# Two first layers: attention by pairs of heads on array halves, and gate rows by a transposition, a store and a broadcasting load

## The chip, the core and the metric

The kernel runs on one core of one Trainium2 chip. Its time is device microseconds of one launch, from inputs in HBM to the output in HBM; the comparison is by medians over several runs. TensorE (PE in the profile) does matmuls, VectorE (DVE), ScalarE (ACT) and GpSimd (POOL) the rest, SyncE (SP) issues most of the loads. All data is float32.

## The reference

Two blocks of two layers each work on x of 256 tokens x 1024 features. The changed parts lie in the first block's layers (0 and 1), and in the residual gates of all four layers (0 to 3).

```python
ada = (cond_act @ w_ada + b_ada)[:, None, :]
sh1, sc1, g1, sh2, sc2, g2 = split(ada, 6)            # each 1024 wide
u = layer_norm(x) * (1 + sc1) + sh1
proj = u @ w_in + b_in                                # p, conv b/c/h, mq mk mv, fq fk fv, f_logit, gates
y_moba = attention of 4 heads of 64 on mq, mk, mv     # causal; with 256 tokens one block: plain softmax
y_fox = attention of 4 heads of 64 on fq, fk, fv      # causal, with a forget bias on the logits
gates = sigmoid(gate_logit)                           # 256 x 4096
merged = sum over n of gates[n] * (branches[n] @ w_branch[n])
x = layer_norm(ALPHA * x + g1 * (merged @ w_o)) * ln1_g + ln1_b
u2 = layer_norm(x) * (1 + sc2) + sh2
x = layer_norm(ALPHA * x + g2 * (square(relu(u2 @ w_up + b_up)) @ w_down)) * ln2_g + ln2_b
```

The second block (layers 2 and 3) has an attention layer with 16 head pairs, then a convolution by spectra (Hyena), each followed by a mixture of 16 experts; its two residual sums are `ALPHA * x + g1 * y` and `ALPHA * x + g2 * f` as well. `g1` and `g2` are one number per feature, the same for every token.

## The kernel before

One program of five queues, each written out in order; engines wait for one another by semaphores. Weights come as pieces of 2 MB (128 partitions x 4096) through a ring of six slots, issued by SyncE in a fixed order; a piece is issued when its slot's last reader is done. PSUM has eight banks: six are taken in turn (`take(pe, name)`), two are held (`take(pe, name, hold)`) for attention outputs and for the modulation sums. `emptied` and `wait_evicted` count a bank's evictions.

Modulation (`ada`) of later layers is computed beside other work: VectorE multiplies a weight piece with the condition vector (`mod_step`, or a quarter of it, `mod_part`), transposes in blocks of 32 and sums (`mod_fold`), TensorE sums over partitions with one small matmul (`modulation`, called a fold below), VectorE adds the bias into `modc` (`mod_evict`). `modc[:, L, j]` has feature p of chunk j on partition p: gates 1 are its columns 16 to 23, gates 2 columns 40 to 47.

**Attention of layers 0 and 1** (`attention(L, extra)` in each engine's block). There are 16 units: two kinds, four heads, two query tiles of 128; tile 0 has 128 keys, tile 1 has 256. They are numbered head by head. A step s issues scores of unit s (contraction over 64 partitions, the half of the array where the head lies), transpositions of the probabilities of unit s-2, values of unit s-3 (64 output partitions), and then one product of the gated merge, `gated_branch(l, s)`: eight matmuls of a weight tile with UT and two with a branch output, 256 columns each. VectorE takes the masked maximum (L1947) and scales the probabilities (L1971), ScalarE exponentiates (L1465) and copies the transposed tile out of PSUM (L1473) and makes the gate (L1486). Gated products 16 to 31 follow the attention; product 16 reads the first attention's output, product 24 the second's. After the last one come the output product (`output_product`), which waits for `merged_ready`, the residual sum and norm on VectorE (`finish_tiles`), and the feed-forward part.

**Gate rows.** The residual sum multiplies a PSUM tile of tokens x features with the gate of each feature, so it needs the gates as a row on all partitions (`grow`). `gate_diag` (VectorE, L1829) writes eight 128x128 diagonal matrices with the gates into `diag`; `gate_rows` (TensorE) multiplies all-ones with it, twice 512 columns, into the two held banks; `gate_rows` (ScalarE, L1419 and L1420) copies them to `grow`, halved for gates 1 of layers 0 and 1, and for gates 2 of layers 2 and 3 also into `gsplit`, where each half of the row lies on 64 partitions. This is done eight times and named (L, i) here, i = 0 for gates 1 and 1 for gates 2:

- (0,0), (1,0): TensorE after gated product 31, ahead of the output product
- (0,1), (1,1): TensorE in the down product, after its fourth piece
- (2,0): ahead of the third layer's attention; (3,0): among the Hyena input products
- (2,1), (3,1): at the start of the mixture, ahead of the router

The mixture then runs a loop over the experts, in which VectorE first writes one-hot columns (L2202) that TensorE's gather needs (tile X), and multiplies by `gsplit` at the end of each expert.

GpSimd issues the loads of the norm's rows (`load_lnrow`, L2508 and L2509) after the previous norm, and computes the pooling windows of layers 0 and 1.

Of the kernel before, what the change touches and what calls it, by code (L numbers as in the profile page):

```python
# [26 lines left out]
P = 128  # L27
D = 1024
N = 256
# [26 lines left out]
PAIRS = 16  # L56
RMS_LIMIT = 2.0 ** 32 / P ** 0.5
# [190 lines left out]
def build(nc, a, out):  # L248
    pieces, place = plan_pieces()
    ctx = ExitStack()  # L250
    with ctx:
# [29 lines left out]
        rstd = sb("rstd", [P, TT])  # L281
        smax = sb("smax", [P, 64])
# [61 lines left out]
        SM2, P2, PT2 = view(7936, 2, 512), view(7936, 4, 512), view(9984, 2, 512)  # L344
# [12 lines left out]
        kspec = nc.dram_tensor("filter_spectra", (P, 2, RING), F32, kind="Internal").ap()  # L357
        ftm = acc
# [39 lines left out]
        diag_ready = sem("gate_diagonal_ready")  # L398
# [160 lines left out]
        def attention_steps(us):  # L559


            for s in range(len(us) + 3):
                yield (s if s < len(us) else None,
                       s - 1 if 0 <= s - 1 < len(us) else None,
                       s - 2 if 0 <= s - 2 < len(us) and us[s - 2]["pair"] != 0 else None,
                       s - 3 if 0 <= s - 3 < len(us) and us[s - 3]["pair"] != 0 else None)

        def attention_tiles(L):
            return (SM1, P1, PT1) if L < 2 else (SM2, P2, PT2)

# [4 lines left out]
        def pairs():  # L575

            us = numbered(2)
            return [us[2 * p:2 * p + 2] for p in range(PAIRS)]

# [31 lines left out]
        def _(pe):  # L611
# [31 lines left out]

            def gate_rows(L, i):

                for h in range(2):
                    g = ("rows", L, i, h)
                    bank = take(pe, g, h)
                    pe.wait_ge(diag_ready, 2 * L + i + 1)
                    finish(mm(bank, C("ones"), diag[:, h * 512:h * 512 + 512], True, True), g)  # L650
# [78 lines left out]
            def attention(L, extra=None):  # L729
                us = numbered(L)  # L730
                for s, _, tr, pv in attention_steps(us):
                    if s is not None:
                        u = us[s]
                        g = ("s",) + u["name"]
                        bank = take(pe, g)
# [14 lines left out]
                    if pv is not None:  # L750
                        u = us[pv]
                        if u["first"]:
                            take(pe, ("o", L, u["name"][1], u["hold"]), u["hold"])
# [1981 lines left out]
```

## Time and profile before

| | |
|---|---|
| median of 3 runs | 2474.4 us (2473.87 to 2475.06) |
| the profiled execution | 2474.91 us, of which the span is 2472.9 |
| PE busy | 2322.6 us, 94% of the span, mean granted clock 0.986 |
| DVE, ACT, POOL busy | 1017.7, 356.3, 31.8 us |
| DMA | 701 MB, mean 283 GB/s; 428 to 430 GB/s in most of the expert loops |

Line 615 is the helper through which nearly all matmuls are issued, so tiles and shapes tell them apart, not the line. In the timeline a row is a run of equal instructions: start, length, engine, line, operation, output and input tiles, shape, count; in brackets the idle time before it and what ended it. A float32 matmul is two instructions. `64*128` is a matmul that contracts over 64 partitions, `128*64` one with 64 output partitions. The last instruction of a run is shown with its full latency, so lengths overlap: the time a run occupies is best read from start to next start.

### The profile page before, as it was taken

What the parts mean: (1) busy time and instruction counts of PE and PEld (TensorE: products, weight loads), DVE (VectorE), ACT (ScalarE), POOL (GpSimd) and SP (SyncE); (2) the same over time, 40 slices, a digit from 0 to 9 for tenths busy, and PEclk for the clock granted to TensorE, in tenths of its full rate; (3) what the DMA queues carried; (4) which work ended last, traced back from release to release, by engine and by line L of the source; (5) the groups of instructions that cost most, each with busy time, mean ns of one, the idle gap of its engine ahead of it and who ended that gap; (6) DMA issues with size and microseconds to landing.
All of it is one profiled execution on the core that took longest, in us unless ns stands there. A gap on an engine that the chain in (4) does not pass through costs nothing.

```text
span 2472.9 us, 26320 instructions
## 1 busy us (share of the span) xinstructions
PE 2322.6 (94%) x10448; PEld 1373.8 (56%) x10448; DVE 1017.7 (41%) x2212; ACT 356.3 (14%) x725; POOL 31.8 (1%) x54
## 2 busy tenths in 40 slices
PE   6999999999999999999998998988899989989997
PEld 5878688458878685467554333333397533333332
DVE  4254656767556567223743111111245521111112
ACT  1211111001211110101532111111100011111111
POOL 0100000002000000000000000000000000000000
PEclk9999999999999999999998999999999989999999
DMA  9644868856267688532045999999954369999996
GB/s 313 255 153 171 306 248 291 305 193 234 98 248 257 218 326 303 187 119 85 35 185 228 430 429 429 428 429 428 417 197 170 122 241 429 429 428 429 428 429 290
DMA packets 160900, 701.04 MB, mean 283 GB/s; under 512 B 6064, under 2 KB 15536, under 8 KB 135216
## 3 DMA queue, kind: packets, MB, share of 16 engines
q1 hardware_dynamic: 158512, 691.49, 70.9%
q0 software_dynamic: 2304, 8.39, 1.0%
q8 instruction: 58, 0.95, 0.2%
q14 instruction: 26, 0.21, 0.0%
HBM read 694.61 MB, written 5.24 MB: 283 GB/s over the span
## 4 chain that ended last, share of the span: by engine, by line
PE 73%; DMA 20%; DVE 3%; ACT 2%; issue 1%; SPq 1%; DVEq 0%; ACTq 0%
PE banks L615 72%; DMA ring<-in_exp_w_down_dram 19%; ACT UT L1406 1%; DMA ring<-in_w_ada_dram 1%; PE banks L680 0%; DVE acc L1790 0%; PE banks L748 0%; DVE acc L1763 0%; ACT arena L1613 0%; SPq L2587 0%; DVE arena L2220 0%; DVE arena L2213 0%; DVE X L1872 0%; PE banks L1153 0%; PE banks L995 0%
## 5 line engine op out<-in xcount | busy, mean ns | idle before, releaser
L615 PE MATMUL banks<-ring,arena 128*64 128x512 f32 (+2 forms) x3776 | 976.4, 593 | 80.0 <-DVE arena L2220 29.1
L615 PE MATMUL banks<-UT,ring 128*128 128x256 f32 (+1 forms) x3696 | 729.3, 356 | 7.0 <-ACT UT L1406 3.9
L615 PEld LDWEIGHTS banks<-ring,arena 128*64 128x64 f32 (+1 forms) x3776 | 360.5, 147 | 660.2 <-issue 619.5
L615 PEld LDWEIGHTS banks<-UT,ring 128*128 128x128 f32 x3696 | 623.7, 192 | 86.9 <-issue 15.9
L1790 DVE SCALAR_TENSOR_TENSOR acc<-ring,cact,acc 128x512 f32<-128x512 f32 x280 | 212.7, 760 | 9.9
L2212 DVE TENSOR_TENSOR arena<-arena,banks 128x512 f32<-128x512 f32 x32 | 33.9, 1061 | 442.0 <-PE banks L615 442.0
L1586 ACT ACTIVATE arena<-banks 128x512 f32<-128x512 f32 (+1 forms) x96 | 65.2, 679 | 799.0 <-PE banks L615 759.9
L615 PE MATMUL banks<-arena 64*128 64x512 f32 (+4 forms) x752 | 139.5, 433 | 4.6 <-ACT arena L1453 2.8
L615 PEld LDWEIGHTS banks<-arena 64*128 64x128 f32 (+2 forms) x752 | 69.1, 172 | 77.9 <-issue 62.1
L2220 DVE TENSOR_TENSOR arena<-banks,acc 128x512 f32<-128x512 f32 x32 | 22.2, 692 | 208.7 <-PE banks L615 208.7
L615 PE MATMUL banks<-ring,XN 128*128 128x512 f32 (+1 forms) x192 | 73.0, 540 | 0.0
L615 PE MATMUL banks<-arena,ring 128*128 128x256 f32 x256 | 65.7, 379 | 0.0
L615 PE MATMUL banks<-X,arena 128*64 128x512 f32 x272 | 64.3, 593 | 1.4 <-DVE arena L2170 1.4
L2213 DVE COPY arena<-banks 128x512 f32<-128x512 f32 x32 | 22.2, 692 | 104.6 <-PE banks L995 104.6
L1883 DVE TENSOR_TENSOR arena<-banks,grow 128x512 f32<-128x512 f32 x24 | 16.6, 690 | 117.4 <-PE banks L615 117.3
L615 PE MATMUL banks<-ring,UT 128*128 128x256 f32 (+2 forms) x256 | 62.6, 394 | 0.0
L615 PE MATMUL banks<-XN,ring 128*128 128x512 f32 (+1 forms) x176 | 60.8, 498 | 0.0
L615 PEld LDWEIGHTS banks<-ring,XN 128*128 128x128 f32 x192 | 34.6, 193 | 38.9 <-issue 38.8
L615 PEld LDWEIGHTS banks<-ring,UT 128*128 128x128 f32 x256 | 46.0, 190 | 13.3 <-issue 8.4
L1549 ACT ACTIVATE arena<-banks,small 128x256 f32<-128x256 f32 x64 | 26.9, 471 | 181.3 <-PE banks L615 181.3
L2095 DVE TENSOR_TENSOR arena<-arena 128x512 f32<-128x512 f32 x32 | 21.8, 687 | 74.9 <-ACT arena L1549 74.9
L615 PEld LDWEIGHTS banks<-arena,ring 128*128 128x128 f32 x256 | 48.6, 190 | 6.6
(249 smaller groups left out, 1453.1 us busy)
## 6 DMA issues: line engine op xcount, KB each, us to landing
ring<-in_exp_w_gate_dram SPq DMA_DIRECT2D x64, 2048.0 KB, 22.1
ring<-in_exp_w_up_dram SPq DMA_DIRECT2D x64, 2048.0 KB, 25.2
ring<-in_exp_w_down_dram SPq DMA_DIRECT2D x64, 2048.0 KB, 17.1
ring<-in_w_in_dram SPq DMA_DIRECT2D x26, 2048.0 KB, 14.0
ring<-in_mod_w_dram SPq DMA_DIRECT2D x24, 2048.0 KB, 9.2
ring<-in_w_ada_dram SPq DMA_DIRECT2D x20, 2048.0 KB, 8.5
ring<-in_w_up_dram SPq DMA_DIRECT2D x16, 2048.0 KB, 9.4
ring<-in_w_down_dram SPq DMA_DIRECT2D x16, 2048.0 KB, 9.3
```

Source lines behind the costliest of these rows:

```text
L615: return nc.tensor.matmul(o, lhs, rhs, start=start, stop=stop)
L1406: x = A(dst[:, k, t * P:t * P + P], bank[:, c * P:c * P + P], ACT.Identity, bias=cols[:, shift + k:shift + k + 1], scale=cols[:, shift + 8 ...
L1549: x = A(rt[:, i % 2, c * N:c * N + N], bank[:, c * N:c * N + N], ACT.Relu, bias=S(f"bup{l}", 2 * i + c, 1))
L1586: A(dst, src, func).then_inc(m["g_evicted"][b], 1)
L1790: link(V.scalar_tensor_tensor(out=dst, in0=w[:, k, :], scalar=cact[:, c0 + k:c0 + k + 1], in1=dst, op0=ALU.mult, op1=ALU.add))
L1883: emptied(V.tensor_tensor(tmp[:, hf, :], bank, grow[:, hf * 512:hf * 512 + 512], ALU.mult), g)
L2095: V.tensor_tensor(HID[:, 2 * i:2 * i + 2, :].rearrange("p c n -> p (c n)"), rt[:, i % 2, :], rt[:, i % 2, :], ALU.mult).then_inc(hid_ready, 1)
L2212: done(V.tensor_tensor(quarters_back(G), by_column(SG), by_column(bank), ALU.mult), "up")
L2213: done(V.tensor_copy(HS.rearrange("p j s -> p (j s)"), start("hidden", e)), "hidden")
L2220: done(V.tensor_tensor(YS, start("down", e), gsplit, ALU.mult), "down")
```

## The change

Attention in layers 0 and 1 works on pairs of heads. The units are numbered so that two heads on the two halves of the partitions, of the same query tile, follow each other. A pair step p issues both units' scores, gated product 2p, both units' transpositions of pair p-1, gated product 2p+1, both units' values of pair p-1, with the two heads' matmuls alternating key tile by key tile. In the ninth step there are no scores; gated products 16 and 17 take the two places, and TensorE waits ahead of them for ScalarE's copy of the first attention's output. VectorE and ScalarE follow the same order.

Gate rows are made without TensorE and ScalarE. VectorE transposes 32 columns of `modc` in blocks of 32 into `grows` (for layers 2 and 3 all four at the start of the third layer). GpSimd stores the eight rows of each of the four blocks to HBM (four stores of 8 x 128 bytes, 4 KB in all), waits for them and for the previous norm, and loads the 4 KB back to all 128 partitions (512 KB); for (2,1) and (3,1) two more loads of 128 KB fill `gsplit`. The halving moves into the residual sum, whose multiplication becomes a three-operand one.

```diff
-                    for h in range(4):
-                        b = (h % 2) * HD
-                        for i in range(TT):
+                    for h2, i, r in itertools.product(range(2), range(TT), range(2)):
+                            h, b = 2 * h2 + r, r * HD
...
+            def head_scores(two):
+                held = [take(pe, ("s",) + u["name"]) for u in two]
+                for bank, u in zip(held, two):
+                    x = mm(bank[:, 0:u["nk"]], u["q"], u["keys"][0][1], True, True)
+                    finish(x, ("s",) + u["name"])
...
+            def head_weigh(l, two):
...
+                for t in range(len(two[0]["values"])):
+                    for u in two:
+                        p0, p1, col = u["at"]
+                        x = mm(bank[p0:p1, col:col + P], u["values"][t], PT1[:, u["n"] % 2, t * P:t * P + P],
+                               t == 0, t == len(u["values"]) - 1)
...
+            def attention(l):                                   # TensorE
+                two = head_pairs(l)
+                for p in range(HEAD_PAIRS + 1):
+                    if p < HEAD_PAIRS:
+                        head_scores(two[p])
+                    else:
+                        wait_evicted(pe, ("o", l, 0, 0))
+                    gated_branch(l, 2 * p)
+                    if p:
+                        head_turn(l, two[p - 1])
+                    gated_branch(l, 2 * p + 1)
+                    if p:
+                        head_weigh(l, two[p - 1])
...
-                attention(l, lambda s: gated_branch(l, s))
-                for i in range(16, 32):
+                attention(l)
+                for i in range(18, 32):
                     gated_branch(l, i)
-                gate_rows(l, 0)
...
+            def attention(l):                                   # ScalarE
...
+                    if p < HEAD_PAIRS:
...                      (exponents of both units)
+                    else:
+                        head_out(l, 0)
+                    gate(l, 2 * p)
...                      (copies of both transposed tiles of pair p-1)
+                    gate(l, 2 * p + 1)
+                head_out(l, 1)
...
+            def attention(l):                                   # VectorE
+                two = head_pairs(l)
+                for p in range(HEAD_PAIRS):
+                    for u in two[p]:
+                        head_largest(u)
+                    if p:
+                        gated_branch(l, 2 * p - 1)
+                    mod_part(MOD_SLOTS["in", l, 5 + p // 2], 2 * (p % 2))
+                    for u in two[p]:
+                        head_probabilities(u)
+                    gated_branch(l, 2 * p)
+                    mod_part(MOD_SLOTS["in", l, 5 + p // 2], 2 * (p % 2) + 1)
+                gated_branch(l, 15)
+                mod_evict(MOD_SLOTS["in", l, 8])
...
-            def gate_diag(L, i):
...
+            def gate_turn(L, i):
+                V.transpose(grows[:, 2 * L + i, :], modc[:, L, 16 * i:16 * i + 32]).then_inc(gate_turned, 1)
...
             def finish_tiles(name, gate, tmp, k, plain=None, between=None):
-                wait_evicted(dve, ("rows",) + gate + (1,))
+                dve.wait_ge(grow_loaded, 16 * (2 * gate[0] + gate[1] + 1))
...
-                        emptied(V.tensor_tensor(tmp[:, hf, :], bank, grow[:, hf * 512:hf * 512 + 512], ALU.mult), g)
+                        emptied(V.scalar_tensor_tensor(out=tmp[:, hf, :], in0=bank, scalar=0.5 if gate in ((0, 0), (1, 0)) else 1.0,
+                                                       in1=grow[:, hf * 512:hf * 512 + 512], op0=ALU.mult, op1=ALU.mult), g)
...
-                wait_evicted(dve, ("rows", L, 1, 1))            # mixture, ahead of the expert loop
+                dve.wait_ge(grow_loaded, 16 * (2 * L + 2))
+                dve.wait_ge(gsplit_loaded, 32 * (L - 1))
...
+            def gate_row(L, i):                                 # GpSimd
+                n = 2 * L + i
+                pool.wait_ge(gate_turned, n + 1)
+                c = 16 + 8 * i
+                row = gate_rows[n].rearrange("(c q n) -> q c n", q=4, n=32)
+                for q in range(4):
+                    G.dma_start(row[q], grows[32 * q + c:32 * q + c + 8, n, :]).then_inc(gate_stored, 16)
+                if n:
+                    pool.wait_ge(x_ready, 2 * n)
+                pool.wait_ge(gate_stored, 64 * (n + 1))
+                G.dma_start(grow[:, :], gate_rows[n].partition_broadcast(P)).then_inc(grow_loaded, 16)
+                if L >= 2 and i:
+                    for h in range(2):
+                        G.dma_start(gsplit[h * CAP:h * CAP + CAP, :],
+                                    gate_rows[n][512 * h:512 * h + 512].partition_broadcast(CAP)).then_inc(gsplit_loaded, 16)
...
                 load_lnrow(2 * L)
                 if L < 2:
                     windows(L)
+                gate_row(L, 0)
                 load_lnrow(2 * L + 1)
+                gate_row(L, 1)
```

All calls of `gate_rows` on TensorE and ScalarE and of `gate_diag` on VectorE are gone. `head_largest` and `head_probabilities` are the two halves of VectorE's old step, for one unit each.

## Rows read from the trace of the kernel before

**Rows 1.** The page: shares of the chain that ended last, by engine.
```profile
PE 73%; DMA 20%; DVE 3%; ACT 2%; issue 1%; SPq 1%; DVEq 0%; ACTq 0%
```

**Rows 2.** Stretches: length, busy us and count of PE, PEld, DVE, ACT, POOL, PEclk, DMA share, GB/s.
```profile
117.20:210.70 93.50, 93.35 (x431) 72.69 (x430) 56.48 (x164) 19.36 (x68) 0.00 (x0) 1.00 0.37 132
210.70:281.00 70.30, 70.13 (x328) 61.77 (x328) 37.05 (x78) 8.17 (x18) 0.00 (x0) 1.00 0.76 280
1327.20:1786.00 458.80, 421.88 (x1952) 151.17 (x1952) 80.15 (x175) 53.13 (x64) 0.00 (x0) 1.00 0.99 418
```

**Rows 3.** Timeline of TensorE in the attention of layer 0.
```profile
132.26 0.70 PE L615 MATMUL banks<-arena 64*128 64x256 f32 x2
132.89 0.44 PE L748 MATMUL banks<-const,arena 128*128 128x128 f32 x2
...
138.14 0.48 PE L615 MATMUL banks<-arena 64*128 64x128 f32 x2
...
143.91 0.70 PE L615 MATMUL banks<-arena 64*128 64x256 f32 x2
```

**Rows 4.** Timeline of TensorE in the attention of layer 2.
```profile
1264.66 1.13 PE L615 MATMUL banks<-arena 64*128 64x256 f32 x8
1265.73 1.98 PE L615 MATMUL banks<-XN,ring 128*128 128x512 f32 x4
1267.55 1.04 PE L1153 MATMUL banks<-const,arena 128*128 128x128 f32 x8
1268.42 1.90 PE L615 MATMUL banks<-UT,ring 128*128 128x512 f32 x4
1270.29 1.09 PE L615 MATMUL banks<-arena 128*64 128x128 f32 x16
1271.32 5.42 PE L615 MATMUL banks<-ring,arena 128*128 128x512 f32 x12
```

**Rows 5.** Timeline of VectorE in the attention of layer 0.
```profile
169.46 0.48 DVE L1804 TENSOR_SCALAR acc<-ring,cact 128x512 f32<-128x512 f32 x1 [5.46 <-DMA ring<-in_w_ada_dram]
```

**Rows 6.** Timelines of TensorE and VectorE at (0,0), and TensorE ahead of the down product.
```profile
280.58 0.29 PE L615 MATMUL banks<-folded,const 128*128 128x16 f32 x2
281.80 0.42 DVE L1986 TENSOR_TENSOR XN<-XN,arena 128x256 f32<-128x256 f32 x1
283.56 3.58 PE L615 MATMUL banks<-diag,const 128*128 128x512 f32 x4 [2.69 <-DVE modc L1742]
286.93 13.62 PE L615 MATMUL banks<-ring,XN 128*128 128x512 f32 x31
...
435.33 4.96 PE L615 MATMUL banks<-ring,arena 128*128 128x512 f32 x11 [1.73 <-DVE arena L2095]
```

**Rows 7.** The stretch of the gate-row matmuls at (0,0).
```profile
283.56:286.93 3.37, 3.37 (x4) 1.31 (x5) 3.23 (x5) 0.60 (x1) 0.00 (x0) 0.54 1.04 405
```

**Rows 8.** Timelines at (0,1), (3,0), (2,0) and (2,1).
```profile
491.01 0.29 PE L615 MATMUL banks<-folded,const 128*128 128x16 f32 x2
...
493.88 6.60 PE L615 MATMUL banks<-ring,arena 128*128 128x512 f32 x15
...
1829.05 1.88 PE L615 MATMUL banks<-diag,const 128*128 128x512 f32 x4
...
1177.43 1.29 DVE L2279 TENSOR_REDUCE smax<-banks 128x1 f32<-128x512 f32 x2
...
1306.56 0.16 DVE L1849 RECIPROCAL rstd<-std 128x1 f32<-128x1 f32 x1 [1.67 <-ACT std L1443]
```

**Rows 9.** GpSimd's loads (x, KB, us to landing: all, at 1800 us), and VectorE's diagonal for (0,0).
```profile
lnrow<-in_ln_g_dram POOLq DMA_DIRECT2D x8, 512.0 KB, 4.1
lnrow<-in_ln_b_dram POOLq DMA_DIRECT2D x1, 512.0 KB, 8.1
255.36 1.65 DVE L1829 TENSOR_SCALAR diag<-const,modc 128x128 f32<-128x128 f32 x8
```

**Rows 10.** Timeline of TensorE in the first expert of layer 2: the gather.
```profile
1342.68 1.89 PE L615 MATMUL banks<-X,arena 128*64 128x512 f32 x8
```

More of the change, by code:

```diff
@@ L557, in build @@
         TURN_BASE = {0: 0, 1: 16, 2: 32}
[L559 to L569, printed above, removed]
         def prob_slot(L, u):
@@ L578, in pairs, with head_pairs @@
             return [us[2 * p:2 * p + 2] for p in range(PAIRS)]
+        def head_pairs(l):
+            us = numbered(l)
+            return [us[2 * p:2 * p + 2] for p in range(HEAD_PAIRS)]
         def turns(p, two):
@@ new lines, in head_scores, with head_turn @@
+            def head_scores(two):
[3 more added lines that the diff above has]
+                    finish(x, ("s",) + u["name"])
+            def head_turn(l, two):
+                for u in two:
+                    g = ("t",) + u["name"]
+                    bank = take(pe, g)
+                    pe.wait_ge(prob_ready, UNIT_BASE[l] + u["n"] + 1)
+                    for k in range(u["nk"] // P):
+                        x = nc.tensor.transpose(bank[:, k * P:k * P + P], P1[:, u["n"] % 4, k * P:k * P + P], C("ident"))
+                    finish(x, g)
@@ new lines, in head_weigh @@
+            def head_weigh(l, two):
+                if two[0]["first"]:
+                    take(pe, ("o", l, two[0]["name"][1], two[0]["hold"]), two[0]["hold"])
+                bank = banks[:, BANKS + two[0]["hold"], :]
+                for u in two:
+                    wait_evicted(pe, ("t",) + u["name"])
+                for t in range(len(two[0]["values"])):
+                    for u in two:
+                        p0, p1, col = u["at"]
+                        x = mm(bank[p0:p1, col:col + P], u["values"][t], PT1[:, u["n"] % 2, t * P:t * P + P],
+                               t == 0, t == len(u["values"]) - 1)
+                if two[1]["last"]:
+                    finish(x, ("o", l, two[1]["name"][1], two[1]["hold"]))
@@ L1408, in modulate_tile @@
                     emptied(x, (name, t, h))
-            def gate_rows(L, i, scale=1.0):
-                if 2 * L + i:
-                    act.wait_ge(x_ready, 2 * (2 * L + i))
-                for h in range(2):
-                    g = ("rows", L, i, h)
-                    bank = filled(act, g)
-                    if L >= 2 and i == 1:
-                        own = slice(h * CAP, h * CAP + CAP)
-                        A(gsplit[own, :], bank[own, :], ACT.Copy)
-                    emptied(A(grow[:, h * 512:h * 512 + 512], bank, ACT.Copy, scale=scale), g)
             def first_share(n):
@@ L2362, in attention_block @@
                 mod_evict(len(MOD_STEPS))
-                gate_diag(2, 0)
+                wait_evicted(dve, ("ada", 3, 11, "x"))
+                for L, i in itertools.product((2, 3), range(2)):
+                    gate_turn(L, i)
                 modulate(("h", 2), UT, 2, 0)
```

191 lines of the change are left out of this document (48 added, 143 removed).

## The prediction, made before the changed kernel had run

> **What bounds the kernel now.** First the page. TensorE is busy 94% of the span and the chain that ended last is 73% TensorE and 20% DMA [rows 1]: the kernel is one line of matmuls, and in parts a line of loads. The table by stretch says which parts [rows 2]. In the attention of layer 0 (117.2 to 210.7 us) TensorE is full at granted clock 1.00 while DMA has a share of 0.37; in the second half of the gated product it is full again, with DMA at 0.76. The expert loop (1327.2 to 1786.0) has DMA at 0.99: it is the loads. There the second expert's loads are issued only when the first expert's products have read their slots, so the loop begins when TensorE gets to it: what TensorE saves ahead of a loop moves the whole loop, and what it saves in a loop is worth nothing. Every edit here is ahead of one.
>
> Next the timeline of TensorE in that attention [rows 3]. Two steps (one unit with 256 keys, one with 128) take from 132.26 to 143.91, 11.65 us. Gated products between other gated products take 70.1/16 = 4.38 us each with their share of the folds [rows 2], 4.33 without. So 11.65 - 8.66 = 3.0 us of two steps is attention. Its instruction time is less: two instructions a matmul, 0.213 us each for 256 columns, 0.107 for 128, is 0.64 for scores, 0.64 for values, 0.32 for three transpositions, 1.6 in all. The other 1.4 us are the joints: each burst has a start of the next 0.15 to 0.2 us later than its instructions need (one score of 256 keys: 132.26 to 132.89 is 0.63 for 0.43).
>
> The pair scheme that the third layer already uses shows what becomes of both [rows 4]: two heads' scores, eight instructions of 256 columns, take 1.06 us from start to start where one after the other would be 8 x 0.213 = 1.70; sixteen value instructions of 128 columns on two halves take 1.03 instead of 1.71; eight transpositions take 0.87.
>
> **The change part by part.** *Attention, per layer.* Before: 93.5 us less 16 x 4.33 leaves 24.2 us that are not gated products (four folds, 0.84, among them). After, for each of 8 pairs: scores are four instructions, of which the second head's first overlaps the first head's last; the 5 slots for 8 of [rows 4] make 3 slots for 4, 0.64 for 256 keys and 0.32 for 128, mean 0.48, plus 0.15 for the joint. Values are 4 or 8 instructions at 1.03/16 = 0.064, mean 0.39, plus 0.15. Transpositions are 2 or 4 at 0.11, mean 0.33. One joint more, 0.15, where a gated product is entered. Sum 1.65, times 8 is 13.2. Folds 0.84. A new wait stands in front of gated product 16: ScalarE can write the first attention's output only after gate 15, which is three operations of 128x256 at 0.47 (page, L1549) after that product's end, 1.4 us, and 0.7 of them lie beside fold and values: 0.7 us idle. Total 14.7, gain 9.5 per layer, **19.0**. Bounds: with no overlap of halves, 1.6 of instructions and four joints of 0.2 are 2.4 per pair, a gain of 3.5; with no joints 8 x 1.2 + 0.84 = 10.4 is left of 24.2, a gain of 13.8. I take 9.5 because all three bursts have a row in the pair scheme. The covers: a pair lasts 10.3 us on TensorE, probabilities are wanted a pair later; VectorE is busy 56.5 us of the stretch [rows 2], 7.1 per pair.
>
> *VectorE's new order* waits in each pair for scores, for exponents and for the first gated product (4.3 us and a gate of 0.47 after the scores). Of its 7.1 us a pair some 3.5 stand behind that last wait, 5.7 us after the scores: done near 9.5, inside 10.3. Once a layer it waits 5.5 us for a weight piece [rows 5]. Queued behind that wait are now a pair's probabilities and a gated sum; TensorE needs the bank of that sum about 11 us after the pair's scores and gets it then. Cost 0, at most 1.
>
> *Gate rows (0,0) and (1,0).* TensorE ends its last fold at 280.8; the gate-row matmul waits for a held bank until 283.56, runs at half clock (0.54 in the window [rows 7]) and the output product starts at 286.93. The sum it needs was done at 281.80 + 0.42 [rows 6]. So the product can start at 282.4: 4.5 us, twice, **9.0**. The idle time left is 1.6 us; after one of 1.73 us eleven matmuls took 4.96, which is full speed [rows 6], so I charge nothing. If the clock fell to 0.54 for the same 3.4 us it would cost 1.6 per layer. VectorE is busy with a modulation step to 291 (before's time); the product's first tile is then ready, and only the second tile's end is on the path.
>
> *(0,1) and (1,1)*: from the fold's end at 491.22 to the next down product at 493.88 [rows 8]: 2.66 us, twice, **5.3**. *(3,0)*: four instructions of 0.427 in an unbroken row of matmuls, **1.7**. *(2,0)*: between 0 and 1.7; I take 0, since VectorE's first maximum there starts with no idle time before it [rows 8], so its own queue sets the time and not the matmul. *(2,1) and (3,1)*: the turning of tile 0 starts 1.72 us earlier; ScalarE then ends its tile 0 and its square root earlier, which VectorE waits 1.67 us for [rows 8]: 1.65 each, **3.3**.
>
> *What is added.* Eight transpositions of 32 columns on VectorE replace 64 products of 0.28 us; neither is on the path. The multiplication with the gate row takes a third operand: 0.69 us in the nearest row, at most 0.76 (L1790 on the page), 24 times, some 10 of them on the path: 0 to 0.7, I take 0.
>
> *The row's way through GpSimd*: four issues of 0.53, a landing, an issue, a landing. The norm rows issued there, 512 KB each, land after 4.1 us in the median (the first of each two), and after 8.1 at the longest [rows 9]. With 8 for each landing: 2.1 + 8 + 0.5 + 8 = 19 us. For (0,0) the columns are there at 255.4, where the diagonal is now written [rows 9], and the first use is at 291: 35 us. (0,1), (1,1), (2,0), (3,0) have over 60. For (2,1) and (3,1) it all starts at the norm's end (1308.0), behind two norm rows, and two half rows follow: 5 + 16 = 21 us. VectorE's wait stands 19 us after that start. Behind it are the one-hot columns, and for them waits TensorE's gather, at 1342.68 [rows 10]: 34 us of cover. Cost 0; landings of 14 us or more would be needed.
>
> The Trainium skill (SBUF — State Buffer, "SBUF: two separate sides") warns that a DMA issued from GpSimd can be held up by VectorE, because its descriptors need a port that some VectorE operations lock; a long hold would be rival (d) below. The landings of 4.1 to 8.1 us, taken while VectorE worked, speak against one that matters. The Trainium skill (TensorEngine Tiling, "Theoretical Speedup") allows up to 2x for halves; the trace has 1.70/1.06 = 1.6. By the page the attention would gain 2.2 us more a layer and the time be 2432.
>
> **Sum:** 19.0 + 9.0 + 5.3 + 1.7 + 3.3 = 38.3. The profiled execution took 2474.9 (span 2472.9 and 2.0 around it), so 2436.6; it lies 0.5 over the median of 2474.4, so 2436.
>
> **Rivals.** (a) *Halves don't overlap in such short bursts.* With only two instructions a head for a score there is one overlap, not three, and the joints may stay. For it: joints are 1.4 of 3.0 us now. Against: 1.03 us for sixteen [rows 4]. Gain 3.5 instead of 9.5 a layer: 2448. (b) *VectorE or a piece of the ring sets the pair.* VectorE's chain of 9.5 is 0.8 under the pair's 10.3, and the 5.5 us wait comes on top once. If the pair stays at 11.6, attention gains nothing: 2455. Against: TensorE waited for neither before, and VectorE's work is the same. (c) *The time saved is waited for at the weights*, in the stretch where DMA has 0.76. For it: the stage is shorter by 4.5 us a layer for the same bytes. Against: no matmul of these stages waits for a load now, and the loads' releases move with TensorE. Worth at most the 9.0 of the merge: 2445. (d) *Slower: the gate row comes late.* Store, wait and load are one chain of two landings on one queue. With L us a landing a row is late by 2.6 + 2L - 35 in (0,0) and (1,0), and by 5 + 2L - 34 in the two mixtures; together 8L - 123. It costs something from L = 14.5 and makes the kernel slower from L = 20; at 25 it is 77 - 38 more than now, 2513. For it: no row shows a small store from GpSimd, and DMA is busy there. Against: 8.1 is the longest landing seen on that queue.
>
> **How the numbers follow.** Forecast 2436 with 0.76 (own range 2428 to 2443); (a) 0.08, (b) 0.06, (c) 0.05, (d) 0.05, of it slower 0.04. The range 2426 to 2454 leaves out part of (b), (d) and the case that joints vanish. A difference under 0.2%, 5 us, is what a measurement can't tell from none. Faster 0.94, within 0.2% 0.02, slower 0.04.
>
> **What would show it.** In the attention, bursts of a pair's scores of about 0.5 and 0.8 us and values of 0.4 and 0.65, and the 16 gated products with all of it in about 84 us, where 93.5 was; the output product 1.6 us after the last fold, at clock 1.00; no matmul on the diagonal but those of the third layer's scaling; both expert loops as long as before; stores and rows on GpSimd's queue landing in under 8 us. Wrong it would be if TensorE had new waits in the attention on VectorE's sums or on a piece, if a pair took over 11 us, or if VectorE stood waiting ahead of the expert loop for the row beyond the first expert's gather.

## The result, and the profile after

| | median us | runs | ratio to before, 95% interval |
|---|---|---|---|
| before | 2474.3 | 2473.87 to 2475.06 (4) | |
| changed | 2435.3 | 2431.75 to 2436.76 (4) | 0.9841 [0.9830, 0.9853] |
| changed, second time | 2434.5 | 2433.69 to 2436.24 (5) | 0.9839 [0.9826, 0.9853] |

Forecast was 2436.0, with a range of 2426 to 2454. The profiled execution of the changed kernel took 2434.49, span 2432.6, 40.3 less than before's span. The chain that ended last has the same shares as in [rows 1]. Where the 40.3 come from is read by starts of the same matmul in both timelines; "forecast" is the prediction's own sum up to that place.

| TensorE starts | before | changed | gained by then | forecast |
|---|---|---|---|---|
| first scores, layer 0 | 117.20 | 117.32 | -0.1 | 0 |
| last fold of the gated product | 280.58 | 269.96 | 10.6 | 9.5 |
| output product | 286.93 | 271.66 | 15.3 | 14.0 |
| down product | 435.33 | 421.68 | 13.7 | 14.0 |
| down product after (0,1) | 493.88 | 477.50 | 16.4 | 16.7 |
| last fold of the gated product, layer 1 | 796.24 | 769.12 | 27.1 | 26.2 |
| output product | 802.72 | 770.81 | 31.9 | 30.7 |
| down product | 950.97 | 920.84 | 30.1 | 30.7 |
| third layer, after (2,0) | 1186.40 | 1153.62 | 32.8 | 33.3 |
| expert loop, layer 2 | 1327.20 | 1292.33 | 34.9 | 35.0 |
| turning behind that loop | 1793.73 | 1757.42 | 36.3 | 35.0 |
| output product, layer 3 | 1945.92 | 1907.28 | 38.6 | 36.7 |
| expert loop, layer 3 | 1999.61 | 1959.17 | 40.4 | 38.3 |

Stretches of the changed kernel, columns as in [rows 2]: the attention up to gated product 18, the rest of the gated product, the expert loop.

```profile
117.32:208.75 91.43, 90.59 (x471) 75.92 (x471) 57.45 (x167) 20.86 (x69) 0.00 (x0) 1.00 0.48 173
208.75:269.96 61.21, 61.21 (x289) 53.98 (x288) 34.57 (x67) 6.99 (x15) 2.62 (x5) 1.00 0.75 275
1292.33:1751.00 458.67, 420.82 (x1954) 150.94 (x1956) 80.82 (x176) 53.12 (x64) 0.00 (x0) 1.00 0.99 420
```

TensorE is as full as before, only with less to do, and the loop is still one of loads. The timeline of TensorE in the attention answers to [rows 3]:

```profile
126.58 0.70 PE L613 MATMUL banks<-arena 64*128 64x256 f32 x4
127.21 3.72 PE L613 MATMUL banks<-UT,ring 128*128 128x256 f32 x16
...
156.72 0.86 PE L613 MATMUL banks<-arena 128*64 128x128 f32 x8
157.51 3.72 PE L613 MATMUL banks<-UT,ring 128*128 128x256 f32 x16
161.07 1.03 PE L613 MATMUL banks<-arena,ring 128*128 128x256 f32 x4
161.93 0.60 PE L733 MATMUL banks<-const,arena 128*128 128x128 f32 x4
162.37 3.62 PE L613 MATMUL banks<-UT,ring 128*128 128x256 f32 x16
...
166.78 1.29 PE L613 MATMUL banks<-arena 128*64 128x128 f32 x12
168.00 3.72 PE L613 MATMUL banks<-UT,ring 128*128 128x256 f32 x16
...
177.97 3.72 PE L613 MATMUL banks<-UT,ring 128*128 128x256 f32 x16
...
197.64 0.44 PE L613 MATMUL banks<-arena 128*64 128x128 f32 x4
198.92 3.69 PE L613 MATMUL banks<-UT,ring 128*128 128x256 f32 x16 [0.84 <-ACT arena L1443]
...
208.16 0.66 PE L613 MATMUL banks<-arena 128*64 128x128 f32 x8
208.75 3.72 PE L613 MATMUL banks<-UT,ring 128*128 128x256 f32 x16
```

Two pairs take 177.97 - 157.51 = 20.46 us, 10.23 each, where two of the old steps took 11.65. Values and scores now share bursts (a row named for its first instruction: x8 is four of values and four of scores of 64x128, x12 is eight and four). Nothing waits in it but product 16, 0.84 us, for ScalarE's copy of the first output (0.7 forecast). The stretch of 91.43 us holds eighteen gated products; less two of 4.33 it is 82.8 for sixteen with the attention, where the prediction has about 84.

At the merge and in the up stage, TensorE's timeline, and under it the stretch behind the wait in the up stage. They answer to [rows 6, 7].

```profile
269.96 0.29 PE L613 MATMUL banks<-folded,const 128*128 128x16 f32 x2
271.66 27.73 PE L613 MATMUL banks<-ring,XN 128*128 128x512 f32 x64 [1.41 <-DVE XN L1936]
...
333.69 0.37 PE L613 MATMUL banks<-folded,const 128*128 128x16 f32 x2 [1.75 <-DVE folded L1728]
...
421.68 13.97 PE L613 MATMUL banks<-ring,arena 128*128 128x512 f32 x32 [1.73 <-DVE arena L2053]
```
```profile
335.00:338.80 3.80, 3.80 (x12) 3.04 (x11) 3.61 (x7) 0.00 (x0) 0.00 (x0) 0.55 0.95 353
```

The output product starts 1.7 us after the fold and takes 27.73 for 64 instructions of 512 columns, 0.433 each; the granted clock was 1.00 in its first 4 us. But the up stage from its wait to the down product takes 421.68 - 333.69 = 87.99 where before had 86.31, behind the same 1.75 us of idle time: TensorE ran 3.8 us at granted clock 0.55 there, which is to say at 1.2 instead of 2.4 GHz for nearly all of it (a half-clock stretch, below). In layer 1 the same, 88.00 for 86.31.

GpSimd's own timeline and its transfers (x, KB, median us to landing), for (0,0) and for (2,1):

```profile
245.23 2.05 POOL L2476 DMA_DIRECT2D gate_rows<-gate_pieces  x4 [168.90 <-DVE gate_pieces L1800]
252.53 0.56 POOL L2480 DMA_DIRECT2D grow<-gate_rows  x1 [5.24 <-DMA gate_rows<-gate_pieces]
...
1273.82 2.00 POOL L2476 DMA_DIRECT2D gate_rows<-gate_pieces  x4
1279.67 0.56 POOL L2480 DMA_DIRECT2D grow<-gate_rows  x1 [3.85 <-DMA gate_rows<-gate_pieces]
1280.22 1.08 POOL L2483 DMA_DIRECT2D acc<-gate_rows  x2
...
grow<-gate_rows POOLq DMA_DIRECT2D x8, 512.0 KB, 6.4
gate_rows<-gate_pieces POOLq DMA_DIRECT2D x32, 1.0 KB, 4.8
acc<-gate_rows POOLq DMA_DIRECT2D x4, 128.0 KB, 3.8
```

In (2,1) the halves land at about 1281.3 + 3.8 = 1285.1; VectorE writes its first columns behind that wait at 1293.46, and TensorE's gather is at 1306.11. The multiplication with the row (L1853) takes 690 ns with its third operand, in the mean of 24.

### The profile page after: what moved, and what is told of

Read it like the earlier page. It is cut to its first block, busy times and chain, and to the rows that moved or that the text cites. A ratio compares the mean times of both kernels' runs of the same rounds, so it can differ in the third digit from the quotient of the medians.

```text
span 2432.6 us, 26231 instructions
## 1 busy us (share of the span) xinstructions
PE 2284.0 (94%) x10416; PEld 1359.6 (56%) x10416; DVE 1005.8 (41%) x2156; ACT 345.4 (14%) x705; POOL 54.5 (2%) x98
## 4 chain that ended last, share of the span: by engine, by line
PE 73%; DMA 20%; DVE 3%; ACT 2%; issue 1%; SPq 1%; DVEq 0%; ACTq 0%
PE banks L613 72%; DMA ring<-in_exp_w_down_dram 19%; DMA ring<-in_w_ada_dram 1%; ACT UT L1400 1%; PE banks L670 0%; DVE acc L1766 0%; DVE acc L1739 0%; ACT arena L1591 0%; SPq L2564 0%; DVE arena L2172 0%; DVE arena L2179 0%; PE banks L1149 0%; PE banks L991 0%; ACT arena L1435 0%; SPq L2640 0%
## 5 line engine op out<-in xcount | busy, mean ns | idle before, releaser
L613 PE MATMUL banks<-arena 64*128 64x512 f32 (+4 forms) x752 | 120.2, 431 | 3.7 <-ACT arena L1435 2.1
L613 PEld LDWEIGHTS banks<-arena 64*128 64x128 f32 (+2 forms) x752 | 59.6, 171 | 69.1 <-issue 55.3
L1475 ACT ACTIVATE arena<-banks,bhalf 128x256 f32<-128x256 f32 x64 | 30.3, 473 | 224.9 <-PE banks L613 224.9
L1853 DVE SCALAR_TENSOR_TENSOR arena<-banks,grow 128x512 f32<-128x512 f32 x24 | 16.6, 690 | 108.6 <-PE banks L613 108.5
```

Source lines behind the costliest of these rows:

```text
L613: return nc.tensor.matmul(o, lhs, rhs, start=start, stop=stop)
L1475: A(gs[:, i % 2, :], bank[:, 0:N], ACT.Tanh, bias=bhalf[:, 32 * l + i:32 * l + i + 1], scale=0.5)\
L1853: emptied(V.scalar_tensor_tensor(out=tmp[:, hf, :], in0=bank, scalar=0.5 if gate in ((0, 0), (1, 0)) else 1.0, in1=grow[:, hf * 512:hf * 5 ...
```

## Experiments

Every kernel below was timed beside the kernel before on the same chip, in five rounds unless said otherwise. "Changed" is 2435.3 and 2434.5 in its two series.

### The two halves of the change by themselves

First the pairs with the old gate rows (the gate-row lines of the diff undone on all four engines):

```diff
+                attention(l)
+                for i in range(18, 32):
                     gated_branch(l, i)
                 gate_rows(l, 0)
```

> The pairs of heads of the changed kernel with the diagonal, the all-ones product and the copies of the kernel before for all eight gate rows. Theory: the pairs alone bring what the attention gained in the changed trace, 10.8 us a layer, 21.6 in all: 2452.8 us, with the gated product's end still waiting for the held bank, about 3.4 us at half clock behind that wait, and the up stage at full clock (84.3 us). Rival: part of the attention's gain comes with the rows (the held banks and ScalarE are freer), then the pairs alone bring the 19.0 of the forecast or less, 2455 or more. If the half-clock stretch of the up stage belongs to the pairs, the up stage lasts 86.0 here too and the kernel stands at 2456.

Then the rows with the old attention:

```diff
                 attention(l, lambda s: gated_branch(l, s))
                 for i in range(16, 32):
                     gated_branch(l, i)
-                gate_rows(l, 0)
```

> The attention of the kernel before with the changed kernel's gate rows (transposition, store, broadcasting load, three-operand sum). Theory: the parts add up; 39.2 of both less 21.6 of the pairs is 17.6: 2456.8 us, with the up stage of layers 0 and 1 at 86.0 us and a half-clock stretch in it, because the one behind the merge is gone. Rival: the up stage's half-clock stretch belongs to the new attention; then it stays at 84.3 here and the rows alone bring 21: 2453.4. Second rival: the gate rows on GpSimd cost something that the pairs hide; then over 2459.

Pairs only: 2453.1 (2449.76 to 2456.86), ratio 0.9912 [0.9898, 0.9925], 21.2 less than before. Rows only: 2458.0 (2455.96 to 2460.97), ratio 0.9932 [0.9918, 0.9945], 16.3 less. The sum, 37.5, is 1.5 to 2 short of what both bring, which the intervals don't tell from additive. In the profile of rows only the up stage has its half-clock stretch (343.85 to 431.85, 88.00 us), so it comes without the new attention. In that of pairs only it is there as well (339.48 to 427.47, 87.99), so it comes without the new rows too; beside it are one at the merge and one at the first scores, and layer 1 has the same three. Both profiles are of the longest of five executions (2460.97 and 2456.86 us), so they say little of how many such stretches the median has. The theory that the merge's wait "takes" the stretch and spares the up stage fell here.

### Where the attention's gain is: overlap or joints

```diff
-                    for h2, i, r in itertools.product(range(2), range(TT), range(2)):
+                    for r, i, h2 in itertools.product(range(2), range(TT), range(2)):
...
-                for t in range(len(two[0]["values"])):
-                    for u in two:
+                for u in two:
+                    for t in range(len(two[0]["values"])):
```

> The changed kernel, but a pair is two heads on the same half of the array (heads 0 and 2, then 1 and 3), and the value matmuls go head after head: the same bursts, joints, waits and instruction counts, with no two neighbouring matmuls on different halves. Theory: overlap of halves is part of the gain: scores of a pair 0.64 for 0.48 us and values 0.64 for 0.39 in the mean, 0.41 a pair, 3.3 a layer, 6.6 in all: 2442 us, and of the 10.8 us a layer 7.5 stay, which are the joints. Rival: halves don't overlap in bursts this short and all of the gain is fewer joints: within 2 us of the changed kernel. Third: most of the gain is overlap and the attention falls back by 8 us a layer or more, 2451.

Measured 2442.4 (2440.61 to 2442.99), ratio 0.9870 [0.9855, 0.9885]: 7.1 more than changed. TensorE's timeline: scores alone, the two bursts that answer to those at 156.72 and 166.78, and the last pair's values:

```profile
127.76 1.13 PE L613 MATMUL banks<-arena 64*128 64x256 f32 x4
128.82 3.72 PE L613 MATMUL banks<-UT,ring 128*128 128x256 f32 x16
...
159.61 1.29 PE L613 MATMUL banks<-arena 128*64 128x128 f32 x8
160.83 3.72 PE L613 MATMUL banks<-UT,ring 128*128 128x256 f32 x16
...
170.10 2.15 PE L613 MATMUL banks<-arena 128*64 128x128 f32 x12
172.18 3.72 PE L613 MATMUL banks<-UT,ring 128*128 128x256 f32 x16
...
213.62 1.09 PE L613 MATMUL banks<-arena 128*64 128x128 f32 x8
214.64 3.72 PE L613 MATMUL banks<-UT,ring 128*128 128x256 f32 x16
```

From start to next start the last three take 1.22, 2.08 and 1.02 us; on two halves it was 0.79, 1.22 and 0.59. With the prediction's 0.213 us for an instruction of 256 columns and 0.107 for one of 128, the instructions of these bursts are 0.85, 1.71 and 0.85 us one after the other. On one half that leaves 0.37, 0.37 and 0.17 for the joints. On two halves half of it, 0.43, 0.85 and 0.43, leaves 0.36, 0.37 and 0.16, the same. So the instructions overlap fully, two heads in the time of one, and the joints stay as they are. Scores alone agree: a pair's four instructions of 256 columns take 1.06 on one half and 0.63 on two, as long as one head's two took before (132.26 to 132.89 [rows 3]). I had expected 3.3 us a layer of overlap, from three slots for four.

From the first scores (118.29) to the merge's last fold (275.85) this kernel takes 157.56, changed 152.64, before 163.38. So of 10.7 us a layer 4.9 are overlap. The other 5.8 come with the pair itself; what changed there is the number of joints, from the full product into a small burst, from kind to kind, and back: 8 in two old steps, 5 in a pair. The rows bear that out: a pair of this kernel takes (182.57 - 160.83) / 2 = 10.87 us, which less two products and half a fold is 2.1, 1.6 of it instructions and 0.5 joints, where two old steps had 1.4. Eight times 0.9, less the 0.6 us that it waits at product 16, is 6.6, an estimate somewhat above the 5.8; no kernel here varies the number of joints alone. Twice 4.9 is 9.8, yet the time differs by 7.1: in the profile this kernel has no half-clock stretch in either up stage (86.31 and 86.30 us), which gives about 3.4 back.

Does the overlap need neighbours on different halves? Only the second part of that edit, with the heads on different halves:

> The changed kernel with the value matmuls of a pair issued head after head and no longer alternating by key tile; heads still lie on different halves. Pairs with one key tile are issued as before, pairs with two are four matmuls, two a head. Theory: two neighbouring instructions overlap only where they lie on different halves, so of a two-tile pair's values only the one place where the heads meet is left: about 0.95 us instead of 0.59, four times a layer, 1.4 a layer, 2.9 in all: 2438 us. Rival: the order doesn't matter, since the other half's instructions overtake anyway: 0.59 stays, 2435. The kernel with both heads on one half (1.02 for this burst) would be the other end.

Measured 2433.6 (2432.33 to 2434.82), ratio 0.9834 [0.9820, 0.9847], no slower than changed. Its last two-tile pair:

```profile
207.53 0.66 PE L613 MATMUL banks<-arena 128*64 128x128 f32 x8
208.13 3.72 PE L613 MATMUL banks<-UT,ring 128*128 128x256 f32 x16
```

0.60 us, where alternation has 0.59. My theory of neighbours was wrong: what counts is that both halves have work in the burst, not the order in which it is issued. By that, the trace agrees with the Trainium skill (TensorEngine Tiling (Array Packing), "Key Properties"), where tiles work independently of one another.

### The merge's wait, and the clock

```diff
                 pe.wait_ge(merged_ready, l + 1)
+                L0, j0, w0 = MOD_STEPS[summed[0] - 1]
+                wait_evicted(pe, ("ada", L0, j0, w0))
```

> The changed kernel with one wait more in layers 0 and 1: ahead of the output product TensorE waits for VectorE's eviction of the last modulation sum, as the gate-row product did, with no matmul added. The idle time ahead of the product grows from 1.4 to 2.65 us a layer. Theory: a half-clock stretch of 3.4 us is paid about once in this part of a layer, at the longest idle time; it comes back behind the merge and leaves the up stage: output product late by 1.25 plus about 1.7, up stage 84.3 for 86.0, together plus 1.25 a layer, 2437.8 us. Rival: both stretches have their own cause; then the merge keeps full clock or drops in addition, the up stage stays at 86.0, and the sum is 2437.8 (no drop) or 2441 (drop).

Measured 2440.3 (2439.56 to 2440.75), ratio 0.9863 [0.9848, 0.9878]: 5.1 more than changed, the rival "both" (2441). Timeline of the output product, then the two stretches behind the waits:

```profile
272.23 29.40 PE L613 MATMUL banks<-ring,XN 128*128 128x512 f32 x64 [2.74 <-issue]
```
```profile
272.23:275.70 3.47, 3.47 (x4) 1.44 (x5) 3.33 (x5) 0.00 (x0) 0.00 (x0) 0.51 1.05 408
337.40:340.90 3.50, 3.50 (x10) 2.80 (x9) 3.33 (x6) 0.00 (x0) 0.00 (x0) 0.55 0.98 366
```

The product costs 29.40 for 27.73 with 2.74 us idle ahead of it, and the up stage keeps its stretch too. So the drop is no debt that is paid once. In the up stage, the same 1.75 us of idle time was followed by a stretch at half clock in 15 of the 22 times that eleven profiles show (two layers each), and cost 1.7 there. It had none in either layer of the kernel before, of the same-half kernel and of the finer waits below, one in the two layers of the long chain, and 14 of 14 in the other seven profiles. Length goes with it: 1.41 us ahead of the output product had none behind it in 16 of 16, 2.7 us had one in 6 of 6. But length isn't all: 1.72 to 1.75 us ahead of the down product had none in 22 of 22. Even one program differs: the long-chain kernel below is the changed one up to the third layer and had none in layer 0.

```profile
334.70:338.50 3.80, 3.80 (x19) 3.36 (x18) 3.61 (x7) 0.00 (x0) 0.00 (x0) 1.00 0.98 365
```

So does the changed kernel itself. In its second profile the first expert's products, behind the same 1.97 us of idle time, take 16.53 us to the gather, at granted clock 0.50 in the first 4.84. In its first profile they take 13.78 (1.00), in the kernel before 15.48 (0.64):

```profile
1290.56:1295.40 4.84, 4.84 (x12) 1.51 (x14) 1.32 (x6) 0.00 (x0) 0.00 (x0) 0.50 0.00 0
```

### How late may the gate row be?

In the two mixtures the stores and their wait are done n times more; three rounds.

```diff
                 pool.wait_ge(gate_stored, ...)
+                if L >= 2 and i:
+                    for again in range(n):
+                        for q in range(4):
+                            G.dma_start(row[q], grows[32 * q + c:32 * q + c + 8, n, :]).then_inc(gate_stored, 16)
+                        pool.wait_ge(gate_stored, ...)
```

> The changed kernel, with the gate row's way lengthened in the two mixtures: ahead of the load GpSimd stores the same eight rows and waits for them twice more. A store with its wait is 2.0 plus 4.8 us, so the halves of the row land some 13.5 us later, near 1299 us in the first mixture, where VectorE reaches its wait at 1292 and TensorE needs the one-hot columns at 1306.1. Theory: the cover ends at the gather of the first expert, so this costs nothing: within 2 us of the changed kernel. Rival: the cover ends where VectorE reaches its wait; then 13.5 less 6.8 is late in each mixture, 13 us in all, 2449.

> The same with six rounds more: the halves land some 40 us later, near 1326 us. Theory: about 21 us of them are free (1285 to 1304 ahead of the gather, and 2 to 3 in which the loads of the second expert still run), so 19 us are late in each mixture: 38 in all, 2473, as much as the whole change brought. Rival: a late row only moves waiting inside the loop, which the loads bound; then under 10 us in all, 2445. Second rival: the loads stop with it and start again only slowly; over 2480.

Two more: 2434.8, ratio 0.9847 [0.9830, 0.9863], no cost. But a further round took 3.3 us, not 6.8, so the halves were issued at 1287.44 for 1280.22, landed near 1292, and VectorE's columns stayed at 1293.46; this run tells nothing of the rival. Six more: 2472.4 (2467.30 to 2476.30, 10 runs), ratio 0.9997 [0.9987, 1.0006]: the whole gain of the change is gone. Its timelines of VectorE and TensorE, its half rows' landing, and TensorE's waits (total, times, longest):

```profile
1304.33 1.08 POOL L2488 DMA_DIRECT2D acc<-gate_rows  x2
1320.66 0.42 DVE L2161 TENSOR_SCALAR arena<-const,arena 128x64 f32<-128x64 f32 x2 [32.39 <-issue]
1321.22 3.67 PE L613 MATMUL banks<-X,arena 128*64 128x512 f32 x8 [18.56 <-DVE arena L2161]
```
```profile
acc<-gate_rows POOLq DMA_DIRECT2D x4, 128.0 KB, 13.8
```
```profile
PE banks L613 <- DVE arena L2161: 35.9, 2, 18.6
```

This kernel's loop begins at 1288.71, 3.62 before the changed one's. So VectorE's columns are 1320.66 - (1293.46 - 3.62) = 30.8 late, the gather 1321.22 - (1306.11 - 3.62) = 18.7, and 12.1 us of lateness were free beyond VectorE's own wait: the cover ends at the gather, as forecast. TensorE's two waits are 35.9 us; the time grew by 37.1 to 37.9. My 40 us of delay came out near (27.7 by the issue and 10.0 by the landing) for another reason than given: rounds were cheaper, but the last wait took 8.14 us and the half rows 13.8 instead of 3.8, since by then the second expert's 2 MB pieces were in flight (DMA share 1.01 in 1300.0 to 1304.3, where the changed kernel had 0.48 in 1280.2 to 1285.0). Here a late row got later.

### A version that beats both

Two edits of TensorE's waits, alone and together, with the changed kernel beside them. The fold of the up stage half a piece later:

```diff
                         pair_feature(("up", l, j, q), w, q * N, UT)
+                        if q == 0:
+                            beside("up", l, j - 1)
                     release(("up", l, j), ("up", l, j, 1))
-                    beside("up", l, j)
+                beside("up", l, 7)
```

and finer waits:

```diff
-                pe.wait_ge(merged_ready, l + 1)
-                output_product(l)
+                output_product(l, lambda k: pe.wait_ge(merged_ready, 8 * l + k + 1))
...
-                pe.wait_ge(hid_ready, 16 * (l + 1))
...
                 def down_piece(j, tiles):
+                    if 0 in tiles:
+                        pe.wait_ge(hid_ready, 16 * l + 2 * j + 2)
```

(VectorE counts the last eight merged chunks singly for it; in `first_pieces` the fold of the second piece is left to the new place.)

> The changed kernel once more, as the measure for the three versions that run beside it: 2435.3 us, within 2.

> The changed kernel, with each small matmul that sums a modulation step in the up stage of layers 0 and 1 issued half a piece later, so that VectorE has it ready. Theory: the 1.75 us that TensorE waits for it after the second piece is gone in each layer, and with it the half-clock stretch behind it (1.7 us): 6.9 us, 2428.4. Rival: the half-clock stretch is owed anyway and comes behind the next idle time (ahead of the down product); then 3.5 us, 2431.8. Slower if VectorE, which now waits for the small matmul half a piece longer, has the squares late for ScalarE: over 2436.

> The changed kernel, with two waits of TensorE counted finer in layers 0 and 1: the output product waits for the merged sum chunk by chunk, the down product for the squares two at a time. Theory: both idle times go, 1.4 and 1.7 us a layer, 6.3 in all: 2429.0; the half-clock stretch in the up stage stays or goes by chance (3.4 less if it goes in both layers, 2425.6). Rival: an idle time that goes is found again ahead of the loops, at the weights: 2434.

> Both edits together. Theory: all four idle times of a layer of this kind go, and with no idle time over 1.5 us left between the attention and the down product but the one ahead of the up stage, no half-clock stretch stands in them: 6.9 + 6.3 = 13.2 us less than the changed kernel, 2422.1, faster than both kernels. Rival: stretches at half clock appear elsewhere instead, 1.7 us each: 2425.5 for two.

| | median us | runs | ratio to before, 95% interval |
|---|---|---|---|
| changed | 2434.5 | 2433.69 to 2436.24 | 0.9839 [0.9826, 0.9853] |
| later fold | 2426.5 | 2426.28 to 2427.59 | 0.9809 [0.9795, 0.9822] |
| finer waits | 2422.7 | 2421.83 to 2424.17 | 0.9791 [0.9777, 0.9804] |
| both | 2422.4 | 2420.74 to 2425.53 | 0.9793 [0.9780, 0.9806] |

The later fold brings 8.0 where idle time is 3.5 (6.9 expected), the finer waits 11.7 where it is 6.3 (6.3 to 9.7 expected). Of the rest 3.4 is clock, the half-clock stretches that left the up stages; where the other 1.1 and 2.0 come from is not shown. In the finer waits' timeline no idle time stands ahead of the output and down products, and the up stage, with its 1.75 us untouched, takes 416.37 - 331.93 = 84.44 to the down product. With the wait of 1.73 that went it would be 86.17, about the 86.31 at full clock:

```profile
269.93 27.71 PE L613 MATMUL banks<-ring,XN 128*128 128x512 f32 x64
...
331.93 0.37 PE L613 MATMUL banks<-folded,const 128*128 128x16 f32 x2 [1.75 <-DVE folded L1728]
...
416.37 13.98 PE L613 MATMUL banks<-ring,arena 128*128 128x512 f32 x32
```

Together they bring hardly more than the finer waits alone (0.3 us), though 3.5 us less is idle. The median is within 0.3 of the theory's 2422.1, but not in the theory's way: its profile has half-clock stretches at the first scores of layers 0 and 1, with no idle time just ahead but with a run of matmuls over 4 and 64 rows:

```profile
114.50 1.99 PE L613 MATMUL banks<-arena,const 4*128 4x256 f32 x8
116.33 0.50 PE L613 MATMUL banks<-const,arena 4*128 4x4 f32 x4
```
```profile
118.00:122.00 4.00, 4.00 (x13) 3.21 (x12) 3.83 (x15) 0.89 (x4) 0.00 (x0) 0.57 0.69 260
609.00:613.70 4.70, 4.70 (x17) 3.76 (x16) 4.26 (x17) 0.89 (x4) 0.00 (x0) 0.64 1.05 390
```

The profile of the finer waits has neither, which is the rival's picture. But the stretch in layer 1 is nothing new. It is there in 10 of all 13 profiles, the kernel before and the changed one among them, and missing in the finer waits, the long chain and the second profile of the changed kernel; the one in layer 0 is in two (both edits, pairs only). The kernel before, then the changed one:

```profile
631.00:635.30 4.30, 4.30 (x13) 3.46 (x13) 3.97 (x14) 0.51 (x3) 0.00 (x0) 0.61 1.05 394
614.70:619.00 4.30, 4.30 (x15) 3.45 (x15) 3.62 (x16) 0.32 (x3) 0.00 (x0) 0.60 1.05 390
```

So the comparison of the last two versions rests on one profile of each, with stretches that come and go in one program. Whether they are chance or follow from where the idle times lie stays open, and with it why the gains of the two edits don't add.

## Why the prediction was right

The median was met within 1 us, and the large terms were met by their mechanisms: overlap and fewer joints in the attention, the gate-row matmuls gone, the row under cover. That it is within 1 us is partly luck. What was not foreseen is +2.5, +0.5, +0.6, +1.4 and +0.3 on one side and -3.4 on the other, and of these the +1.4 and the -3.4 come and go with the clock between profiles of one program.

- **Attention** (forecast 9.5 a layer, bounds 3.5 to 13.8): 10.7 and 10.8. The bursts are as forecast or shorter (scores 117.32 to 117.74 and 126.58 to 127.21, 0.42 and 0.63 us for 0.5 and 0.8; last values 0.59 for 0.65). What was oversized is the pair: 10.23 less two gated products of 4.33 and half a fold of 0.21 is 1.46 us where the sum has 1.65; eight times 0.19 is 1.5, less 0.14 for the longer wait at product 16. Values of a pair and scores of the next but one are one burst, 0.79 and 1.22 us where the sum's parts make 0.88 and 1.45. Behind that is a misread row. The 1.06 us for eight score instructions [rows 4] were read as five slots, "5 slots for 8", and 1.70/1.06 as an overlap of 1.6. Read like the rows of the same-half kernel they are four slots (0.85) and one joint (0.2), an overlap of 2, so the sum put part of the joint into the slots and then added the joint again. (The 2.2 us a layer that the prediction gives for an overlap of 2 come to 1.8 with its own terms.) The claim that halves overlap is shown by the same-half kernel, 4.9 us a layer.
- **Merge** (4.5 each, no clock drop): 4.7 and 4.8, at full clock. Charging nothing was right, in 16 of 16, but the reason given was weak: a row after 1.73 us at one place (the down product, which had no drop in 22 of 22) says little of another, as the up stage shows.
- **The missed term**: the up stage is 1.7 us longer in each layer by half clock behind an idle time that was there before. I had looked for clock only where the change touches the queue. Against the sum it is -3.4. Why it came is open: up to there the changed kernel, its second profile and the two chain kernels are one program and have it in 7 of 8 layers, and each half of the change has it by itself, but of the kernel before there is one profile, with 0 of 2.
- **(0,1), (1,1)**: 2.7 each, as forecast. **(2,0)**: 0, as forecast; the scores start some 2 us earlier, and the next step waits 2.29 us for VectorE's sums. **(2,1), (3,1)**: 1.7 each at the router. **(3,0)**: 2.3 for 1.7; the other 0.6 was not followed up.
- **Not in the forecast either**: the first expert loop is 1.4 us shorter. Before, its first 4.8 us ran at 0.64, now at 1.00. That is not the change's: in the changed kernel's second profile they ran at 0.50. And TensorE's half clock in the third layer and the router moved, +1.1 and -0.8. All together: 38.3 + 2.5 (attention) + 0.5 (merge) - 3.4 + 0.3 + 1.4 + 0.6 is 40.2; the spans differ by 40.3.
- **GpSimd's chain**: cost 0, as forecast. Landings were under 8 us, the halves land 12.6 us after the norm's end (1272.5) where I allowed 21, and the cover was 33.6 for 34. Of some 38 us of delay 19 were free, where 21 of 40 were expected. The long-chain kernel shows that rival (d) was a real one: with halves 38 us later in each mixture the kernel stands at the time of before. The prediction has that point for the mixtures and the merges together, at landings of 20 us; the merges were not tried.
- **Third operand**: 0; 690 ns against 690.

Rival (a) is refuted by the same-half kernel, (b) by the pair period of 10.23 us without a wait for VectorE or a piece, (c) by the output product, which starts with its weights there.

## What to carry to other kernels

Two heads of 64 belong in one burst on the two halves of the array: half of the gain is overlap, which needs no alternation, and half comes with the pair, in which small matmuls are entered and left less often. To price such a burst from a row, take the joint out first (here 0.16 to 0.2 us where the full product follows): what is left halves. A wait of TensorE costs its idle time and, behind 1.75 us often and behind 2.7 us always here, 1.7 us more at half clock, so such waits in a full stretch are worth a finer count or a later place: here 3.5 to 6.3 us of idle time gave 8 to 12. A row brought by a store and a broadcasting load is free while it lands ahead of the first reader's reader; measure that cover from both ends, since a transfer that is late can meet traffic that makes it later, as here (13.8 us for 3.8). And don't read a difference of 2 or 3 us between two profiles as the edit's before a second profile of the same program has shown the same.

## What the runs showed of the hardware that was not expected

- The order of a burst's matmuls between two halves doesn't matter: eight instructions, four on each, take 0.60 us head after head, 0.59 alternating, and 1.02 all on one half. Joints aside the overlap is full: four score instructions on two halves take 0.63 us, as long as two on one.
- Of TensorE's clock: it fell from 2.4 to 1.2 GHz behind 1.75 us of idle time in 15 of 22 cases and not in 7, in the same program both ways; behind 1.41 us it stayed up in 16 of 16, behind 2.7 us it fell in 6 of 6. Behind 1.73 us ahead of the down product it stayed up in 22 of 22. It also fell with no idle time just ahead, behind matmuls over 4 and 64 rows (0.57 in 118.00:122.00 of both edits), at that place of layer 0 in 2 of 13 profiles and of layer 1 in 10 of 13.
- GpSimd's stores of 1 KB: four issues take 2.0 us, the first wait for them 3.4 to 7.1 us, a repeated one 1.3 to 1.9; the last ones of the long chain took 7.6 and 8.1. A broadcast of 128 KB takes 3.8 us, and 13.8 beside 2 MB loads.
